# Second mixer of a two-block network: attention in pairs of heads, the dilated half beside the cross projections, rotary scores on 128 rows

## The chip, the cores and the metric

The kernel runs on one NeuronCore of a Trainium2 chip. The metric is the device time of one execution in microseconds. PE is TensorE, DVE VectorE, ACT ScalarE, POOL GpSimd, SP the queue that issues most DMAs.

## The reference

Two blocks run one after the other over 256 latent tokens of width 1024, all in float32. The change touches only the mixer of the second block, which starts by one wide projection and then has two kinds of attention, eight heads each; their outputs are joined, projected and added:

```
proj = h @ w_in                       # h = rmsnorm(x), 1024 -> 3008 columns
q_nope, q_rope, c_kv, k_rope, q_idx, k_idx, w_idx, qkv = split(proj)   # rope() on q_rope, k_rope, q_idx, k_idx
q_lat = einsum('bshn,hnc->bshc', q_nope, w_uk)
index = einsum(relu(q_idx . k_idx), w_idx)        # 8 index heads, causal
sel   = top_k(index, 64)                          # per query
s     = (q_lat . c_kv[sel] + q_rope . k_rope[sel]) * 96 ** -0.5
o_a   = (softmax(s) @ c_kv[sel]) @ w_uv           # sparse attention, 8 heads
# dilated attention, 8 heads of 64: windows (128,1), (512,4), (2048,16), causal,
# the three outputs weighted by the softmax of their log denominators
o_b   = dilated_attention(rope(q_b), rope(k_b), v_b)
x     = x + concat(o_a, o_b) @ w_out
# then: cross attention over 256 memory tokens, an MLP, a final norm
```

With weights from the log denominators, the dilated attention is one softmax over all causal keys in which a key counts as often as it lies in a window.

## The kernel before

Activations stand transposed, features on the 128 partitions and tokens in the free dimension. All large projections go through one stream of weight blocks (128 x 1024 float32, 512 KB). SP loads block n + 4 once DVE is done with block n; ACT copies a block to a rounded high part (`split`, L1434), DVE subtracts for the low part (`low`, L1890), and PE adds three products, high x high, high x low, low x high (`tile`, L597 to L599, 24 matmuls of 256 columns; `moving`, L1038 to L1040, 12 of 512 columns). ACT and DVE prepare a block three blocks ahead (`lead`). Every engine has its own program, and within an engine everything runs in the order in which the code is written; semaphores join the engines. So the order of the work is what each of the four programs says.

The second mixer goes in five stretches:

- `in2`: 22 tiles of the input projection, copied by ACT into `proj` (PJ);
- `in2_v`: four blocks for the dilated values, then the norm of the latent `kv2`;
- a loop over `SIDE` = 16 weight blocks, eight for the cross keys (`xk`) and eight for the cross values (`xv`). Beside the blocks stand, by the step j: two rotations (`rotate`, L1053) at j under 8, four index products (L1144) with ACT's relu and DVE's weighted sum at j = 4 to 7, top-k rounds on DVE (L2414 to L2417) at j = 8 to 15, latent queries (L1152) at j = 10 to 13;
- `attend(DSA)`: the sparse attention, 16 steps, one head and 128 queries each;
- `attend(DIL)`: the dilated attention, 16 steps.

A step a of `attend` is: PE the scores of a (L1162 and L1163, or L1185), the transposes of the probabilities of a - 2 (L1077), the values of a - 3 (L1169 or L1190); DVE scale and mask (L2354), maximum (L2356), negation (L2357), then for a - 1 the reciprocal and the scaling of the probabilities (L2365, L2366); ACT the exponential (L1789, L1787) and the copy of the transposed probabilities (L1795). In the dilated attention DVE also multiplies by the count of windows and sums (L2364). A step always takes all 256 keys. The rotary part of the sparse scores has 32 features, so its product uses 32 rows of PE; four heads lie above each other in one tile, and so does the rotary key, four times:

```
mm(o[:, 0:SEQ], QL[:, h, q], PJ[:, 6, :], start=True, stop=False)
return mm(o[:, 0:SEQ], PJ[po:po + 32, 4 + h // 4, q], PJ[po:po + 32, 7, :], start=False, stop=True)
```

The last stretch is followed by the output projection `out2`, which takes each 128 features when their low part is there.

## Time and profile before

| | |
|---|---|
| runs | 1772.07, 1773.58, 1779.05 us (median 1773.58) |
| profiled execution | 1773.6 us, its span 1771.7 us |
| PE busy | 1664.0 us (94%), 11578 matmuls |
| DVE, ACT, POOL busy | 1145.7 (65%), 800.2 (45%), 111.4 us (6%) |
| chain that ended last | PE 85%, DVE 8%, ACT 3%, issue 2%, DMA 1% |
| DMA | 230.72 MB, mean 130 GB/s |

The share of PE is an average over stages that differ. A window gives, for one stretch, how long each engine was busy and the mean granted clock of PE, where 1.00 is 2.4 GHz and 0.50 is 1.2 GHz. A busy PE at 0.50 does half the work of one at 1.00. Each timeline row is an instruction, or several alike merged, with its start and length; matmuls overlap, so what one costs is the distance between starts. In brackets stands how long the engine was idle before, and for whom.

### The profile page before, as it was taken

How to read it: one execution, taken by the hardware profiler on the slowest of the kernel's cores; microseconds unless marked ns; L12 is line 12 of the kernel's file. 1: busy time of each engine (PE TensorE's matmuls, PEld its weight loads, DVE VectorE, ACT ScalarE, POOL GpSimd, SP SyncE). 2: the span in 40 equal slices, each digit the busy share in tenths (PEclk: the TensorE clock that was granted, in tenths of full speed). 3: DMA queues.
4: the chain of work that ended last, by engine and by line, in shares of the span. 5: the costliest groups of instructions: out<-in, count | busy, mean ns of one | idle time of the engine just before them, and what ended most of it. 6: DMA issues, size and time to landing. Idle time of an engine off the chain costs nothing.

```text
span 1771.7 us, 31774 instructions
## 1 busy us (share of the span) xinstructions
PE 1664.0 (94%) x11578; PEld 1420.7 (80%) x11578; DVE 1145.7 (65%) x2011; ACT 800.2 (45%) x1434; POOL 111.4 (6%) x124
## 2 busy tenths in 40 slices
PE   7999968888989999999899999999999999999998
PEld 1688867788867777788786699999987557899998
DVE  0678464455489999966545468875559665567643
ACT  2556422223354444422364457764444434556542
POOL 1000033040100000001000010001000001010000
PEclk9999888889989999999899999999999877999999
DMA  8355310000245555555342045566453202345553
GB/s 351 112 189 193 103 31 2 1 3 1 84 131 186 181 184 183 178 181 175 122 143 72 1 127 186 186 207 209 145 176 111 68 1 84 108 134 187 189 188 96
DMA packets 62841, 230.72 MB, mean 130 GB/s; under 512 B 6753, under 2 KB 8033, under 8 KB 62241
## 3 DMA queue, kind: packets, MB, share of 16 engines
q1 hardware_dynamic: 61344, 223.37, 38.8%
q0 software_dynamic: 1120, 5.80, 1.0%
q8 instruction: 61, 1.00, 0.2%
q10 hardware_dynamic: 288, 0.33, 0.1%
q14 instruction: 28, 0.22, 0.0%
HBM read 228.43 MB, written 1.05 MB: 130 GB/s over the span
## 4 chain that ended last, share of the span: by engine, by line
PE 85%; DVE 8%; ACT 3%; issue 2%; DMA 1%; POOL 0%; DVEq 0%; ACTq 0%; SPq 0%; POOLq 0%
PE proj L597 21%; PE proj L599 20%; PE proj L598 20%; PE bank L1077 1%; DVE w_low L1890 1%; DMA a_first<-a_head 1%; PE bank L649 1%; PE proj L672 1%; PE bank L1190 1%; PE bank L843 1%; PE bank L860 1%; PE bank L1185 1%; PE bank L1096 1%; PE proj L1038 1%; PE bank L863 1%
## 5 line engine op out<-in xcount | busy, mean ns | idle before, releaser
L597 PE MATMUL proj<-h_high,w_high 128*128 128x256 f32 (+1 forms) x1768 | 583.2, 330 | 22.7 <-DVE h_low L1923 12.3
L599 PE MATMUL proj<-h_high,w_low 128*128 128x256 f32 (+1 forms) x1768 | 573.5, 324 | 0.0
L598 PE MATMUL proj<-h_low,w_high 128*128 128x256 f32 (+1 forms) x1768 | 573.2, 324 | 0.0
L1890 DVE TENSOR_TENSOR w_low<-w_raw,w_high 128x1024 fp32r<-128x1024 f32 x322 | 393.2, 1224 | 221.2 <-ACT w_high L1434 219.9
L1434 ACT ACTIVATE w_high<-w_raw 128x1024 fp32r<-128x1024 f32 x322 | 338.1, 1055 | 244.7 <-PE proj L599 237.4
L597 PEld LDWEIGHTS proj<-h_high,w_high 128*128 128x128 f32 x1768 | 338.9, 192 | 65.3 <-issue 18.9
L599 PEld LDWEIGHTS proj<-h_high,w_low 128*128 128x128 f32 x1768 | 339.4, 192 | 27.3
L598 PEld LDWEIGHTS proj<-h_low,w_high 128*128 128x128 f32 x1768 | 338.9, 192 | 25.5
L599 PE MATMUL proj<-act_high,w_low 128*128 128x256 f32 (+1 forms) x608 | 189.9, 312 | 0.0
L597 PE MATMUL proj<-act_high,w_high 128*128 128x256 f32 (+1 forms) x608 | 189.4, 311 | 0.4 <-DVE w_low L1890 0.4
L598 PE MATMUL proj<-act_low,w_high 128*128 128x256 f32 (+1 forms) x608 | 189.5, 312 | 0.0
L597 PEld LDWEIGHTS proj<-act_high,w_high 128*128 128x128 f32 x608 | 114.1, 188 | 8.2 <-DVE w_low L1890 0.8
L598 PEld LDWEIGHTS proj<-act_low,w_high 128*128 128x128 f32 x608 | 113.8, 187 | 7.7
L599 PEld LDWEIGHTS proj<-act_high,w_low 128*128 128x128 f32 x608 | 114.3, 188 | 6.6
L1510 ACT ACTIVATE conv_in<-proj 128x512 f32<-128x512 f32 (+1 forms) x100 | 49.9, 499 | 118.9 <-PE proj L599 115.9
L2008 DVE SCALAR_TENSOR_TENSOR mod_products<-a_ring,cond_rows 128x1024 f32<-128x1024 f32 x80 | 103.0, 1287 | 0.0
L1321 POOL TENSOR_TENSOR tmp<-tmp 128x256 f32<-128x256 f32 (+1 forms) x40 | 44.2, 1111 | 893.7 <-ACT tmp L1450 715.8
L2008 DVE SCALAR_TENSOR_TENSOR a_ring<-a_ring,cond_rows 128x1024 f32<-128x1024 f32 x80 | 97.5, 1219 | 0.0
L1972 DVE SCALAR_TENSOR_TENSOR conv_mid<-conv_in,cols_sb,conv_mid 128x512 f32<-128x512 f32 (+1 forms) x100 | 63.5, 635 | 14.0 <-DVE conv_mid L1970 8.2
L1970 DVE SCALAR_TENSOR_TENSOR conv_mid<-conv_in,cols_sb,conv_mid 128x512 f32<-128x512 f32 (+1 forms) x100 | 63.2, 632 | 11.6 <-ACT conv_mid L1511 9.9
L1511 ACT ACTIVATE conv_mid<-proj,cols_sb 128x512 f32<-128x512 f32 (+1 forms) x100 | 58.8, 588 | 0.0
L1642 ACT ACTIVATE lev_m<-bank 128x256 f32<-128x256 f32 (+1 forms) x48 | 18.3, 384 | 87.7 <-PE bank L843 63.6
(382 smaller groups left out, 2048.8 us busy)
## 6 DMA issues: line engine op xcount, KB each, us to landing
w_raw<-w_stream SPq DMA_DIRECT2D x322, 512.0 KB, 3.6
a_ring<-a_stream SPq DMA_DIRECT2D x80, 512.0 KB, 3.7
a_first<-a_head SPq DMA_DIRECT2D x4, 2048.0 KB, 20.2
x<-x_in SPq DMA_DIRECT2D x1, 2048.0 KB, 13.3
late_tab<-late_tables POOLq DMA_DIRECT2D x1, 1664.0 KB, 7.6
cond_rows<-cond_rows SPq DMA_DIRECT2D x1, 1024.0 KB, 18.6
cond_rows<-cond_rows POOLq DMA_DIRECT2D x1, 1024.0 KB, 5.1
x<-mem_in POOLq DMA_DIRECT2D x1, 1024.0 KB, 6.0
```

The lines of the kernel that those rows point to most:

```text
L597: mm(out_, wh, xh, start=first, stop=False)
L598: mm(out_, wh, xl, start=False, stop=False)
L599: return mm(out_, wl, xh, start=False, stop=last)
L1321: nc.gpsimd.tensor_tensor(squares(name, 0), squares(name, 0), squares(name, k), ALU.add).then_inc(n_early, 1)
L1434: f(wh(n), RAW[:, n % 4, :], ACT.Copy).then_inc(w_high, 1)
L1510: f(XP[:, k % 2, 0:n, 1:SEQ + 1], PL[t % 2][:, 0:width].rearrange("p (s t) -> p s t", s=n), ACT.Copy)
L1511: f(C1[:, k % 2, 0:width], PL[t % 2][:, 0:width], ACT.Identity, scale=C[:, ds(taps + 3 * k + 1 + 3 * per * it, 1)]).then_inc(tile_out, 1)
L1642: f(M1[x, k % 2, :, :], BK[k % 2][x, 0:4 * 64].rearrange("p (h j) -> p h j", h=HEADS), ACT.Copy).then_inc(G["lv_m1"], 1)
L1890: v.tensor_tensor(wl(n), RAW[:, n % 4, :], wh(n), ALU.subtract).then_inc(w_low, 1)
L1970: v.scalar_tensor_tensor(o, XP[:, k % 2, 0:n, 0:SEQ], C[:, ds(taps + 3 * k + 3 * per * it, 1)], o, ALU.mult, ALU.add).then_inc(conv_mid, 1)
L1972: v.scalar_tensor_tensor(o, XP[:, k % 2, 0:n, 2:SEQ + 2], C[:, ds(taps + 3 * k + 2 + 3 * per * it, 1)], o, ALU.mult, ALU.add).then_inc(con ...
L2008: v.scalar_tensor_tensor(o, w, 1.0, cond[:, s, :], ALU.mult, ALU.mult, accum_out=MODF[:, ds(2 * (A_FIRST + j) + s + 2 * off, 1)]).then_inc ...
```

## The change

- The columns of the input projection are put in another order: index queries, index key and weights first, then latent, rotary parts, dilated queries and keys, and the sparse queries last. A rotation follows each of the input tiles from m = 2 on, two tiles behind (`rope_at`). The norm's second half, the index products in pairs and the transpose of the latent go beside the four `in2_v` blocks; the other index products and the latent queries beside the first four cross-key blocks.
- Both attentions go two heads per step (`PairLayer`, `pair_step`), eight steps each; steps of the first 128 queries take only 128 keys. The index sums and top-k rounds do the same.
- The top-k rounds move to j = 4 to 11, and the dilated attention is placed beside the blocks from j = 4 (`DIL_AT`). The sparse attention is alone behind them.
- The count of windows goes into the mask as its logarithm, and DVE's product and the table of counts go.
- The rotary key is copied by POOL into four tiles that are zero outside of 32 rows (`KM`); the rotary scores take all 128 rows of a query tile against the copy of their head.
- `out2` waits for all heads of the sparse attention at once.

```diff
-                           rows(np.where(count > 0, 0, NEG)), rows(count)], axis=1).astype(f)
+                           rows(np.where(count > 0, np.log(np.maximum(count, 1)), NEG))], axis=1).astype(f)
...
-    w_in2 = np.concatenate([w2[:, 0:896], np.tile(w2[:, 896:928], (1, 4)), np.tile(w2[:, 1440:1504], (1, 2)),
-                            wide(w2[:, 1504:1512]), w2[:, 928:1440], w2[:, 1512:2536]], axis=1)
+    w_in2 = np.concatenate([w2[:, 928:1440], np.tile(w2[:, 1440:1504], (1, 2)), wide(w2[:, 1504:1512]), w2[:, 768:896],
+                            w2[:, 512:768], np.tile(w2[:, 896:928], (1, 4)), w2[:, 1512:2536], w2[:, 0:512]], axis=1)
...
+        KM = place("rope_key_rows", [P, 4, SEQ])
...
+        SX = place("scores", [P, 2, 2, SEQ])
...
+        class PairLayer:
+
+            def __init__(self, name, a0, e0, scale):
+                self.name, self.a0, self.e0, self.scale = name, a0, e0, scale
+                self.n, self.per, self.lag = 8, 4, 9 if name == "dsa" else 7
+                self.steps = self.n - self.per + self.lag + 1
+
+                self.pairs = [(0, 4), (1, 5), (2, 6), (3, 7)] if name == "dsa" else [(0, 2), (1, 3), (4, 6), (5, 7)]
...
         SIDE = 16
-        ROTATE_AT = {j: [r for r in (2 * j, 2 * j + 1) if r < len(ROPE2)] for j in range(SIDE)}
-        INDEX_AT, TOP_AT, LATENT_AT = range(4, 8), range(8, 16), range(10, 14)
+        TOP_AT, DIL_AT = range(4, 12), 4
...
+            def pair_step(ly, a, scores, values):
...
+                if a < ly.n:
...
+                    pe.wait_ge(A["at_m"], ly.a0 + max(0, a - 1))
+                    for i in range(2):
+                        last = scores(ly.pairs[a // 2][i], a % 2, BK[a % 2][:, i * SEQ:i * SEQ + (1 + a % 2) * P])
+                    last.then_inc(A["at_s"], 1)
+                if 2 <= a < ly.n + 2:
+                    p = a - 2
+                    nk = 1 + p % 2
+                    pe.wait_ge(A["at_n"], ly.a0 + p + 1)
+                    for i in range(2):
+                        for k in range(nk):
+                            at = i * SEQ + k * P
+                            last = nc.tensor.transpose(BK[2 + p % 2][:, (i * nk + k) * P:(i * nk + k + 1) * P], PB[:, p % 3, at:at + P], ID[:])
+                    last.then_inc(A["at_t"], 1)
+                if 3 <= a < ly.n + 3:
+                    p = a - 3
+                    e, nk = p // 2, 1 + p % 2
+                    pe.wait_ge(A["at_pt"], ly.a0 + p + 1)
...
+                    for i in range(2):
+                        last = values(ly.pairs[e][i], p % 2, PT[:, p % 2, i * nk:(i + 1) * nk, :], nk)
+                    last.then_inc(A["at_o"], 1)
...
+            def dil_scores(h, qt, o):
+                q, po = slice(qt * P, (qt + 1) * P), 64 * (h % 2)
+                return mm(o, PJ[po:po + 64, QB + h // 2, q], PJ[po:po + 64, KB + h // 2, 0:(1 + qt) * P], start=True, stop=True)
+
+            def dil_values(h, qt, pt, nk):
+                po, at = 64 * (h % 2), h // 2 % 2 * SEQ + qt * P
+                for k in range(nk):
+                    last = mm(BK[4 + h // 4][po:po + 64, at:at + P], VBK[:, k, h * 64:(h + 1) * 64], pt[:, k, :], start=(k == 0), stop=(k == nk - 1))
+                return last
...
+            def index_logits(b):
+
+                for c in index_at(b):
...
+                    po, w = 64 * (h % 2), (1 + c // 8) * P
+                    if c >= 2:
+                        pe.wait_ge(A["ix_r"], c - 1)
+                    mm(index_bank(c)[:, 0:w], PJ[po:po + 64, QI + h // 2, qt * P:(qt + 1) * P], PJ[po:po + 64, KI, 0:w], start=True, stop=True).then_inc(A["ix_l"], 1)
...
+            first_tiles("in2", LAT, SEQ, h_ready("mix"))
+            for m in range(2, 22):
                 tile(B0["in2"] + m, T0["in2"] + m, LAT, SEQ)
-            moving("in2_v", HH, HL, SEQ, range(4), 2, 4)
-            norm("kv2")
+                rotate(ROPE2, r1, rope_at(m))
...
+            norm_sum("kv2")
+            for b in range(4):
+                moving("in2_v", HH, HL, SEQ, (b,), 2, 4)
+                if b == 0:
+                    norm_spread("kv2")
+                if b == 2:
+                    pe.wait_ge(n_xn, NORM_C0["kv2"] + 1)
+                    for qt in range(2):
+                        last = nc.tensor.transpose(BK[5][:, qt * P:(qt + 1) * P], PJ[:, LAT_KV, qt * P:(qt + 1) * P], ID[:])
+                    last.then_inc(A["ct_t"], 1)
+                index_logits(b)
...
+                index_logits(4 + j)
+                if j < 4:
...
+                if j >= DIL_AT:
+                    pair_step(DIL, j - DIL_AT, dil_scores, dil_values)
...
+            pe.wait_ge(A["km_done"], 4)
...
+                q, k = slice(qt * P, (qt + 1) * P), slice(0, (1 + qt) * P)
+                mm(o, QL[:, h, q], PJ[:, LAT_KV, k], start=True, stop=False)
+                return mm(o, PJ[:, QR + h // 4, q], KM[:, h % 4, k], start=False, stop=True)
...
+            def dsa_out(pair):
...
+                pe.wait_ge(A["ol_out"], pair + 1)
+                po = 64 * (pair % 2)
+                for i in range(2):
+                    last = mm(PL[pair // 2][po:po + 64, i * SEQ:(i + 1) * SEQ], WUV[:, DSA.pairs[pair][i], :], OL[:, pair % 2, i, :], start=True, stop=True)
+                last.then_inc(A["ol_o"], 1)
+
+            for a in range(DSA.n + 3):
+                pair_step(DSA, a, dsa_scores, dsa_values)
+                if a >= 6 and a % 2 == 0:
+                    dsa_out((a - 6) // 2)
+            dsa_out(3)
+
+            project("out2", LAT, SEQ, lambda k: (A["at_y"], DSA.e0 + 2))
...
+            nc.gpsimd.memset(KM[:], 0.0).then_inc(A["km_zero"], 1)
+            pool.wait_ge(A["km_zero"], 1)
+            pool.wait_ge(A["rp_d"], len(ROPE1) + ROPE2_TILES.index(KRP) + 1)
+            for i in range(4):
+                rows = slice(32 * i, 32 * i + 32)
+                nc.gpsimd.tensor_copy(KM[rows, i, :], PJ[rows, KRP, :]).then_inc(A["km_done"], 1)
...
+            def pair_step(ly, a, out_bank, out_chunk):
+                if a < ly.n:
+                    r, w = a % 3, (1 + a % 2) * P
+                    act.wait_ge(A["at_m"], ly.a0 + a + 1)
+
+                    act.wait_ge(A["at_t"], ly.a0 + max(0, a - 2))
+                    for i in range(2):
+                        last = f(PB[:, r, i * SEQ:i * SEQ + w], SX[:, a % 2, i, 0:w], ACT.Exp, bias=SA[:, 1, r, i:i + 1], accum_out=SA[:, 2, r, i:i + 1])
+                    last.then_inc(A["at_p"], 1)
+                if 2 <= a < ly.n + 2:
+                    p = a - 2
+                    nk = 1 + p % 2
+                    act.wait_ge(A["at_t"], ly.a0 + p + 1)
+                    act.wait_ge(A["at_o"], ly.a0 + p - 1)
+                    f(PT[:, p % 2, 0:2 * nk, :], BK[2 + p % 2][:, 0:2 * nk * P].rearrange("p (k q) -> p k q", k=2 * nk), ACT.Copy).then_inc(A["at_pt"], 1)
...
+                if j >= DIL_AT:
+                    pair_step(DIL, j - DIL_AT, lambda e: BK[4 + e][:].rearrange("p (c q) -> p c q", c=2), lambda h, e: h[:, 4 + 2 * e:6 + 2 * e, LAT])
+            for a in range(DSA.steps):
+                pair_step(DSA, a, lambda e: PL[e][:].rearrange("p (c q) -> p c q", c=2), lambda h, e: h[:, e:e + 3:2, LAT])
...
+            def pair_step(ly, a, out_bank, out_chunk, mask):
+                if a < ly.n:
+                    r, w = a % 3, (1 + a % 2) * P
+                    sx = SX[:, a % 2, :, 0:w]
+                    dve.wait_ge(A["at_s"], ly.a0 + a + 1)
+                    link(v.scalar_tensor_tensor(sx, BK[a % 2][:].rearrange("p (i k) -> p i k", i=2)[:, :, 0:w], ly.scale, mask(a % 2)[:, 0:w].unsqueeze(1).to_broadcast([P, 2, w]), ALU.mult, ALU.add))
+                    link(v.tensor_reduce(SA[:, 0, r, :], sx, AXES.X, ALU.max))
+                    v.tensor_scalar(SA[:, 1, r, :], SA[:, 0, r, :], -1.0, None, ALU.mult).then_inc(A["at_m"], 1)
+                if 1 <= a <= ly.n:
+                    p = a - 1
+                    r, w = p % 3, (1 + p % 2) * P
+                    dve.wait_ge(A["at_p"], ly.a0 + p + 1)
+                    link(v.reciprocal(SA[:, 3, r, :], SA[:, 2, r, :]))
+                    pb = PB[:, r, :].rearrange("p (i k) -> p i k", i=2)[:, :, 0:w]
+                    v.tensor_tensor(pb, pb, SA[:, 3, r, :].unsqueeze(2).to_broadcast([P, 2, w]), ALU.mult).then_inc(A["at_n"], 1)
...
                 if j == TOP_AT[0]:
                     dve.wait_ge(A["ix_a"], 16)
...
                 if j in TOP_AT:
 
-                    v.max(M8[:, 0, :], IX[:, 0, :])
+                    v.max(M8[:, 0, :], IX[:, 0, 0:P])
                     link(v.max(M8[:, 1, :], IX[:, 1, :]))
-                    v.match_replace(IX[:, 0, :], M8[:, 0, :], IX[:, 0, :], TAKEN)
+                    v.match_replace(IX[:, 0, 0:P], M8[:, 0, :], IX[:, 0, 0:P], TAKEN)
                     link(v.match_replace(IX[:, 1, :], M8[:, 1, :], IX[:, 1, :], TAKEN))
...
+                if j >= DIL_AT:
+                    pair_step(DIL, j - DIL_AT, lambda e: BK[4 + e][:].rearrange("p (c q) -> p c q", c=2), lambda h, e: h[:, 4 + 2 * e:6 + 2 * e, LAT],
+                              lambda qt: ltab("dneg", qt))
+            for a in range(DSA.steps):
+                pair_step(DSA, a, lambda e: PL[e][:].rearrange("p (c q) -> p c q", c=2), lambda h, e: h[:, e:e + 3:2, LAT], lambda qt: AM[:, qt, :])
```

The names in the listings that follow are tiles: `w_high` and `w_low` the parts of a weight block, `probs` the probabilities, `bank` and `proj` PSUM banks (`proj` as a source is PJ). ACT beside cross-key blocks before, two steps of the loop with index work:

```order
L1434 ACTIVATE w_high<-w_raw 128x1024
L1834 ACTIVATE cross_k<-proj 128x256
L1850 ACTIVATE relu<-bank 128x256 x4
L1434 ACTIVATE w_high_145<-w_raw 128x1024
L1834 ACTIVATE cross_k<-proj 128x256
```

ACT beside cross-key blocks now, from j = 6:

```order
L1946 ACTIVATE cross_k<-proj 128x256
L1880 ACTIVATE probs,pair_small<-scores,pair_small 128x128 x2
L1887 ACTIVATE probs_t<-bank 128x256
L1511 ACTIVATE w_high_147<-w_raw 128x1024
L1946 ACTIVATE cross_k<-proj 128x256
L1880 ACTIVATE probs,pair_small<-scores,pair_small 128x256 x2
L1887 ACTIVATE probs_t<-bank 128x512
```

The exponentials and the copy of the dilated attention now stand between two weight blocks.

DVE beside a cross-value block before, one top-k round between two blocks:

```order
L1890 TENSOR_TENSOR w_low<-w_raw,w_high 128x1024
L2414 MAX max_137<-index 128x8
L2415 MAX max_137<-index 128x8
L2416 MATCH_REPLACE index<-max_137,index 128x256
L2417 MATCH_REPLACE index<-max_137,index 128x256
L1890 TENSOR_TENSOR w_low_146<-w_raw,w_high_145 128x1024
```

DVE now, beside a block at j = 4 to 11:

```order
L1996 TENSOR_TENSOR w_low_148<-w_raw,w_high_147 128x1024
L2543 MAX max_137<-index 128x8
L2544 MAX max_137<-index 128x8
L2545 MATCH_REPLACE index<-max_137,index 128x128
L2546 MATCH_REPLACE index<-max_137,index 128x256
L2476 SCALAR_TENSOR_TENSOR scores<-bank,late_tab 128x512
L2477 TENSOR_REDUCE pair_small<-scores 128x2
L2478 TENSOR_SCALAR pair_small<-pair_small 128x2
L2483 RECIPROCAL pair_small<-pair_small 128x2
L2485 TENSOR_TENSOR probs<-probs,pair_small 128x2x128
L1996 TENSOR_TENSOR w_low<-w_raw,w_high 128x1024
```

Five instructions of a dilated step stand behind the top-k round and ahead of the next block.

PE in the sparse attention before, one step:

```order
L1162 MATMUL bank<-proj,q_lat 128x256
L1163 MATMUL bank<-proj 128x256
L1077 MATMUL bank<-ident_sb,probs 128x128 x2
L1169 MATMUL bank<-probs_t,c_tok 128x128 x2
L1162 MATMUL bank<-proj,q_lat 128x256
```

PE now, one step of two heads:

```order
L1242 MATMUL bank<-proj,q_lat 128x256
L1243 MATMUL bank<-rope_key_rows,proj 128x256
L1242 MATMUL bank<-proj,q_lat 128x256
L1243 MATMUL bank<-rope_key_rows,proj 128x256
L1129 MATMUL bank<-ident_sb,probs 128x128 x4
L1248 MATMUL bank<-probs_t,c_tok 128x128 x2
```

Two heads' scores stand together; the values behind them are of an earlier step with 128 keys.

## Rows read from the trace of the kernel before

**Rows 1.** Windows of the second mixer's five stretches: us, busy time (count) by engine, PEclk the granted clock.
```profile
1243.30:1307.80 64.50, 64.50 (x528) 64.49 (x529) 34.58 (x43) 31.78 (x49) 0.00 (x0) 0.96 0.53 164
1307.80:1322.40 14.60, 12.78 (x61) 10.19 (x60) 5.14 (x7) 7.24 (x12) 0.00 (x0) 1.00 0.63 184
1322.40:1387.60 65.20, 62.63 (x372) 50.41 (x370) 57.18 (x127) 28.82 (x53) 0.00 (x0) 1.00 0.39 128
1387.60:1434.20 46.60, 45.28 (x176) 26.07 (x176) 25.84 (x90) 18.40 (x60) 0.00 (x0) 0.82 0.04 12
1434.20:1480.10 45.90, 42.59 (x130) 23.37 (x129) 31.00 (x116) 13.89 (x36) 0.00 (x0) 0.56 0.00 1
```

**Rows 2.** Windows of 4 us, and one of the first mixer's attention.
```profile
970.00:975.00 5.00, 5.00 (x24) 2.73 (x25) 1.99 (x5) 1.96 (x6) 0.00 (x0) 1.00 0.01 3
1384.00:1388.00 4.00, 3.27 (x15) 2.31 (x13) 3.90 (x12) 2.70 (x4) 0.00 (x0) 1.00 0.38 131
1392.00:1396.00 4.00, 4.00 (x12) 2.22 (x11) 2.43 (x8) 1.30 (x5) 0.00 (x0) 0.50 0.00 0
1412.00:1416.00 4.00, 4.00 (x20) 2.28 (x19) 2.46 (x10) 1.42 (x6) 0.00 (x0) 1.00 0.00 0
...
1456.00:1460.00 4.00, 4.00 (x12) 2.02 (x12) 2.22 (x9) 0.83 (x3) 0.00 (x0) 0.50 0.00 0
```

**Rows 3.** Timeline of PE in an index tile: start, us, engine, line, what, [idle before].
```profile
1340.25 1.02 PE L1053 MATMUL bank<-proj,late_tab 128*128 128x256 f32 x4
1341.20 0.70 PE L1144 MATMUL bank<-proj 64*128 64x256 f32 x4
1342.37 0.97 PE L1144 MATMUL bank<-proj 64*128 64x256 f32 x4 [0.47 <-ACT relu L1850]
...
1346.20 1.03 PE L1053 MATMUL bank<-proj,late_tab 128*128 128x256 f32 x4
```

**Rows 4.** Timeline of DVE beside the cross values.
```profile
1382.88 1.23 DVE L1890 TENSOR_TENSOR w_low<-w_raw,w_high 128x1024 fp32r<-128x1024 f32 x1 [0.79 <-ACT w_high L1434]
1384.03 0.42 DVE L2414 MAX8 max<-index 128x8 f32<-128x256 f32 x1
...
1385.72 1.22 DVE L1890 TENSOR_TENSOR w_low<-w_raw,w_high 128x1024 fp32r<-128x1024 f32 x1
```

**Rows 5.** Timeline of DVE in the sparse attention.
```profile
1390.73 0.42 DVE L2354 SCALAR_TENSOR_TENSOR scores<-bank,top_mask 128x256 f32<-128x256 f32 x1
...
1391.64 0.15 DVE L2357 TENSOR_SCALAR small<-small 128x1 f32<-128x1 f32 x1
```

**Rows 6.** Timeline of ACT beside the values and in the sparse attention.
```profile
1384.20 1.06 ACT L1434 ACTIVATE w_high<-w_raw 128x1024 fp32r<-128x1024 f32 x1 [1.42 <-PE proj L1040]
...
1427.69 0.51 ACT L1789 ACTIVATE probs<-scores,small 128x256 f32<-128x256 f32 x1 [1.47 <-DVE small L2357]
...
1428.20 0.36 ACT L1795 ACTIVATE probs_t<-bank 128x256 f32<-128x256 f32 x1
```

**Rows 7.** Instructions by form, first mixer's attention: line, what, xcount | busy, mean ns | idle.
```profile
L1795 ACT ACTIVATE probs_t<-bank 128x512 f32<-128x512 f32 x15 | 8.8, 588 | 0.0
...
L2356 DVE TENSOR_REDUCE small<-bank 128x1 f32<-128x512 f32 x11 | 7.6, 692 | 13.3 <-PE bank L1092 13.3
```

**Rows 8.** Timeline of PE in the sparse attention at full clock.
```profile
1412.99 0.70 PE L1162 MATMUL bank<-proj,q_lat 128*128 128x256 f32 x2
1413.62 0.69 PE L1163 MATMUL bank<-proj 32*128 32x256 f32 x2
1414.24 0.44 PE L1077 MATMUL bank<-ident_sb,probs 128*128 128x128 f32 x2
1414.52 0.61 PE L1169 MATMUL bank<-probs_t,c_tok 128*128 128x128 f32 x4
1414.96 0.60 PE L1162 MATMUL bank<-proj,q_lat 128*128 128x256 f32 x2
1415.49 0.69 PE L1163 MATMUL bank<-proj 32*128 32x256 f32 x2
```

More of the change, by code:

```diff
@@ L440, in two_blocks_kernel @@
         PT = place("probs_t", [P, 2, 4, P])
-        SX = place("scores", [P, 2, SEQ])
+        SX = place("scores", [P, 2, 2, SEQ])
         RT = place("rot", [P, 2, SEQ])
@@ L1062, in _, with attend @@
             pe.wait_ge(tile_out, T0["out1"] + 2)
-            def attend(ly, scores, values, extra=None):
+            def attend(ly, scores, values):
                 nb = len(ly.banks)
@@ L1165, in dsa_values @@
-            def dsa_values(h, qt, pt):
-                if qt == 0 and h >= 2:
-                    pe.wait_ge(A["ol_out"], h - 1)
-                for k in range(2):
-                    last = mm(BK[4 + h % 2][:, qt * P:(qt + 1) * P], CTK[:, k, :], pt[:, k, :], start=(k == 0), stop=(k == 1))
-                return last
-            def dsa_out(h):
-                pair, po = h // 2, 64 * (h % 2)
-                pe.wait_ge(A["ol_out"], h + 1)
-                if h % 2 == 0 and pair >= 2:
-                    pe.wait_ge(A["at_y"], DSA.e0 + pair - 1)
-                mm(PL[pair % 2][po:po + 64, 0:SEQ], WUV[:, h, :], OL[:, h % 2, :], start=True, stop=True).then_inc(A["ol_o"], 1)
@@ L1822, in _ @@
             norm_high("mix")
-            project("in2", copy_to("in2", PJF, SEQ), 5)
-            for m in (20, 21):
+            for m in range(22):
                 split(B0["in2"] + m + lead("in2"))
@@ L1827, in _, with index_relu @@
                 f(PJ[:, m, :], PL[(T0["in2"] + m) % 2][:, 0:SEQ], ACT.Copy).then_inc(tile_out, 1)
[L1828 to L1829 removed]
+            def index_relu(b):
+                for c in index_at(b):
+                    w = (1 + c // 8) * P
+                    act.wait_ge(A["ix_l"], c + 1)
+                    if c >= 2:
+                        act.wait_ge(A["ix_a"], c - 1)
+                    f(RL[:, c % 2, 0:w], index_bank(c)[:, 0:w], ACT.Relu).then_inc(A["ix_r"], 1)
+            norm_start("kv2")
+            square("kv2", 0, (tile_out, T0["in2"] + LAT_KV + 3))
+            for b in range(4):
+                split(B0["in2_v"] + b + lead("in2_v"))
+                if b == 0:
+                    norm_root("kv2")
+                if b == 3:
+                    for m in range(2):
+                        t = T0["in2_v"] + m
+                        done(t)
+                        f(VBK[:, m, :], PL[t % 2][:], ACT.Copy).then_inc(tile_out, 1)
+                    act.wait_ge(A["ct_t"], 1)
+                    f(CTK[:], BK[5][:, 0:SEQ].rearrange("p (k c) -> p k c", k=2), ACT.Copy).then_inc(A["ct_out"], 1)
+                index_relu(b)
             for j in range(SIDE):
@@ L2409, in _ @@
+                index_sum(b)
+            for j in range(SIDE):
+                low((B0["xk"] + j if j < 8 else B0["xv"] + j - 8) + lead("xk"))
+                index_sum(4 + j)
                 if j == TOP_AT[0]:
                     dve.wait_ge(A["ix_a"], 16)
-                    link(v.tensor_tensor(IX[:], IX[:], causal, ALU.add))
+                    for qt in range(2):
+                        ins = v.tensor_tensor(IX[:, qt, 0:(1 + qt) * P], IX[:, qt, 0:(1 + qt) * P], causal[:, qt, 0:(1 + qt) * P], ALU.add)
+                    link(ins)
```

249 lines of the change are left out of this document (116 added, 133 removed).

## The prediction, made before the change was run

> **What bounds the kernel now.** I read the page first (busy shares and the chain that ended last), then the windows by stage, and last the timelines of single engines. On the page PE is 94% busy and 85% of the chain. The second mixer runs from 1243.3 to 1480.1 us, 236.8 us in five stretches [rows 1]: the input projection (64.5), its value block with the latent norm (14.6), the cross keys and values with rotations, indexer and latents beside them (65.2), the sparse attention (46.6) and the dilated attention (45.9). The reader is to see that in the last two PE is busy 45.28 and 42.59 us while its granted clock averages 0.82 and 0.56: they are bound by PE at half clock. In 4 us pieces the clock is 0.50 with PE busy all 4 us, goes back to 1.00 in the middle of the sparse attention, and never in the dilated one [rows 2]. ACT's exponentials wait for DVE (1.47 us ahead of one [rows 6]), but PE runs through that time, so it costs nothing.
>
> The profiled execution took 1773.6 us, 1.9 more than its span of 1771.7, and equals the median of the runs (1773.58). I sum against 1773.6.
>
> **The input projection, 64.5 to 72.2.** Its 22 tiles stay. Sixteen rotations come in after the tiles. Two of them take 0.95 us on PE (1340.25 to 1341.20 [rows 3]), so 16 x 0.48 = 7.7 is added. DVE has 1.15 for a weight block [rows 4] and three steps of a rotation, each like the 0.42 of [rows 5], 2.4 of a tile's 3.4 us, so it stays hidden; without that cover each tile would wait for DVE.
>
> **Values and norm, 14.6 to 16.1.** The second half of the norm moves behind a weight block; of the 1.8 us that PE is idle there (14.6 less 12.78 [rows 1]) I take 1.2 as gone. It waits for the sum until DVE has scaled eight chunks of x, which is no worse than before. Added are eight index products of 128 columns. With 256 columns four took 2.07 less a stall of 0.47 (1341.20 to 1343.3 [rows 3]), 0.40 each; with half the columns between 0.20 and 0.40, I take 0.25, so 2.0, and 0.7 for transposes that came later before.
>
> **The first four cross-key tiles, 18.0.** A tile is 2.9 (1343.3 to 1346.20 [rows 3]); two index products and two latents of the same 64-row form at 0.40 come on top: 4.5 each. The chain of four index products with a 0.47 us stall per tile [rows 3] is gone; that, and half the columns for the first 128 queries, is where this part gains.
>
> **The other twelve tiles, with the dilated attention and the top-k beside them, 64.** PE's own work is 12 x 2.9 = 34.8 and the attention of 8 pair steps: scores 4 x (0.6 + 1.1), transposes 3.3, values 4 x (0.6 + 1.2), all between the 64-row products of [rows 3] and the 128-row ones of [rows 8] with something for the 64 columns, together 17.3, so 52.1. But I find a new loop between DVE and ACT, which is longer. ACT makes the high half of a weight block, DVE its low half, DVE then does a top-k round, the masked scores, maximum and negation; ACT must take the exponentials of these and copy transposed probabilities before it comes to the next weight block. Nothing of this overlaps within the loop:
> - DVE's weight block and top-k round are 2.84 from start to start (1382.88 to 1385.72 [rows 4]); for the first 128 queries the round now has 128 columns, and at the 0.27 that lies between 256 and 512 elements of a maximum [rows 5, 7] two instructions save 0.27: 2.57.
> - Scores, maximum, negation: 1.06 for 256 elements (1390.73 to 1391.79 [rows 5]). For 512 the maximum takes 0.692 where 256 took 0.42 [rows 5, 7], so 1.6.
> - ACT: an exponential with its sum is 0.51 for 256 (1427.69 to 1428.20 [rows 6]), I take 0.40 for 128; two are 1.02 or 0.80. The transposed copy holds ACT for 0.29 after 128x256, 0.53 after 128x512 (0.588 against 0.36 [rows 6, 7]). The next high half is 1.06 [rows 6]. With two handovers 2.2 or 2.7.
> Even to odd step: 2.2 + 2.57 + 1.6 = 6.4; odd to even: 2.7 + 2.57 + 1.06 = 6.3. PE needs 4.3 to 5.9 per tile here and waits, through the normalized probabilities, for that loop. The first maximum comes about 5.9 us after the stretch begins, seven loops are 44 less 0.8 for the copies that the first two lack, and from the last maximum PE has about 14.3 (four tiles 11.6, last values and transposes, and a wait on the mask): 63.5, I say 64. Bounds: 52.1 if everything hides, and 12 x 6.4 = 77 if every tile is held.
>
> **The sparse attention alone, 31.7.** Two heads share a step. From the stretch at full clock [rows 8]: a 256-column score product 0.63, and 0.53 at its best (1414.96 to 1415.49), I take 0.55 and 0.30 for 128 columns, so four even steps of 4 x 0.30 and four odd ones of 4 x 0.55 are 13.6; 24 transposes at 0.14 are 3.3; 24 value products at 0.22 are 5.3; 8 output products at 0.58 are 4.6. Sum 26.8. Idle: 1.2 at the start for the copies of the cross values, 1.2 until the first probabilities, 1.0 in the tail, and 1.5 before the output projection, which now waits for all its heads and not one by one. DVE's 2.0 to 2.4 per step is under PE's 3.3. The four padded copies are made on POOL, idle here, and their wait ended long before. At half clock the 26.8 would be up to 53.6.
>
> The product with 32 rows took 0.63 and the one with 128 rows beside it 0.63 (1412.99, 1413.62, 1414.24 [rows 8]), so the padding takes nothing off a product as such. The Trainium skill ("TensorEngine Tiling (Array Packing)", Key Properties) says that a change of tiling mode drains TensorE. By it the 32-row product also slowed its neighbour and the all-128-row scores would run at 256 columns in the best 0.53 or a little under; the sum would be 31 instead of 31.7. I do not use it.
>
> **Sum.** 72.2 + 16.1 + 18.0 + 64 + 31.7 = 202.0 against 236.8: -34.8. Nothing before or after the mixer changes but names and counts, and a table that is 256 KB shorter. 1773.6 - 34.8 = 1738.8, say 1739.
>
> **Rivals.** (a) *The loop doesn't hold PE.* The twelve tiles take 52.1: 1727. For it: weights are made three blocks ahead. Against: scores are needed in the same tile, only the weights are ahead; and before, a like exchange between ACT and DVE already held index tiles to one every 5.95 us for 5.5 of PE's work [rows 3]. (b) *The clock falls in the sparse attention*, as it did by 1392 [rows 2]. For it: a start with two idle stretches of 1.2. Against: the first mixer's attention, 128-row and 64-row products of 512 columns, ran at 1.00 throughout [rows 2], and the 32-row products are gone. It costs 8 if the first half of the stage goes at half clock, 26.8 if all: 1747 to 1766, I say 1752. (c) *Slower than before: the clock falls beside the tiles and stays down.* The place is the first dilated steps, where a tile is followed by 64-row products and up to 1.8 us of waiting. At half clock a tile is 5.8 and the attention 4.2: 10.0 x 8, and 29 for the last four, 109 instead of 64; the sparse stage then also starts low, +26.8: +72, 1811. It decides for slower from +34.8, that is with three quarters of the tiles at half clock. Against it: at 1384 to 1388 with PE busy only 3.27 and at all projection tiles the clock is 1.00 [rows 2], and the index tiles with 64-row products and stalls had 1.00 as well [rows 1]. A short fall in some tiles, +6 to +16 (1745 to 1755), is likelier than this.
>
> The Trainium skill ("TensorE: Matmul & The Clock Gate", Why this matters for your kernels) asks that matmuls follow each other without long pauses to keep the full clock. By that rule (b) and (c) could not happen, since no pause is long; this trace disagrees, with 0.50 at PE busy 4.00 of 4.00 us [rows 2]. So I leave (b) its chance.
>
> **Numbers.** Forecast 1739, with its own range 1732 to 1746, chance 0.45; (a) 0.17; (b) 0.20; a short fall beside the tiles 0.14; (c) 0.03; the rest 0.01 near no change. Eight in ten lie between 1723 (rival (a) with a little less in the sparse stage) and 1758 (rival (b) at more than its middle). What a measurement here can tell from no change is 0.5%, 8.9 us, so faster means below 1764.7: all cases but (c), the rest and the far end of (b). Faster 0.95, same 0.02, slower 0.03.
>
> **What would show it.** The five stretches of the profile after should be near 72, 16, 18, 64 and 32. Tiles beside the dilated scores should come every 6.3 to 6.4 us, with PE waiting 1 to 2 us before a transpose for the probabilities, DVE idle 1.5 to 2 us before its weight block for ACT, and ACT idle only before exponentials. A period of 5 means (a). A granted clock under 0.9 in the last stretch means (b), under 0.8 in the fourth the fall beside the tiles. The forecast is wrong if the fourth stretch is under 57 or over 71, or the last over 38.

## The result, and the profile after

The changed kernel took 1738.34 us (median of four, 1736.91 to 1740.02) against 1773.83 (four runs, 1772.07 to 1779.05) for the kernel before; ratio 0.978, 95% interval 0.976 to 0.980. The forecast was 1739. The profiled execution took 1738.19 us with a span of 1736.0. The mixer runs from 1242.52 to 1444.05 us: 201.5 instead of 236.8. Its five stretches, cut as those of [rows 1] (us, busy time and count of PE, its weight loads, DVE, ACT, POOL, then granted clock, DMA share, GB/s):

```profile
1242.52:1314.45 71.93, 71.93 (x562) 70.86 (x562) 51.30 (x89) 31.52 (x50) 2.43 (x4) 0.96 0.48 154
1314.45:1330.94 16.49, 14.79 (x75) 11.29 (x75) 8.83 (x16) 7.12 (x17) 0.00 (x0) 1.00 0.40 128
1330.94:1347.24 16.30, 16.30 (x129) 14.26 (x129) 8.38 (x12) 10.09 (x26) 0.00 (x0) 1.00 0.40 130
1347.24:1411.28 64.04, 54.99 (x298) 42.27 (x296) 43.45 (x109) 27.85 (x65) 0.00 (x0) 0.97 0.31 100
1411.28:1444.05 32.77, 24.81 (x154) 19.85 (x153) 17.14 (x43) 15.91 (x49) 0.00 (x0) 1.00 0.04 14
```

| stretch | before | forecast | after |
|---|---|---|---|
| input projection | 64.5 | 72.2 | 71.9 |
| values, norm | 14.6 | 16.1 | 16.5 |
| first four cross tiles | in 65.2 | 18.0 | 16.3 |
| twelve tiles with top-k and dilated attention | in 65.2, and 45.9 | 64 | 64.0 |
| sparse attention | 46.6 | 31.7 | 32.8 |

The two attentions, which ran at 0.82 and 0.56 before, now run at 1.00 and, between the tiles, 0.97. One short fall is left; two windows of 4 us with it, and one of the sparse attention, answer to [rows 2]:

```profile
1364.00:1368.00 4.00, 2.19 (x12) 1.46 (x11) 2.50 (x7) 2.36 (x7) 0.00 (x0) 0.90 0.36 128
1368.00:1372.00 4.00, 4.00 (x13) 2.94 (x12) 3.83 (x12) 0.36 (x1) 0.00 (x0) 0.67 0.39 130
...
1416.00:1420.00 4.00, 2.90 (x19) 2.65 (x20) 3.34 (x10) 2.24 (x9) 0.00 (x0) 1.00 0.02 6
```

The clock fell near 1367, after PE had waited 1.35 and 1.81 us in two steps, and was back by 1371. It cost some 1.7 us (a tenth of 4 and a third of 4), an estimate from these two windows.

The loop that the forecast found is there. Start, length, engine, line, and in brackets the idle time before and whom it was for; the second turn, from one negated maximum of the dilated scores to the next:

```profile
1359.32 0.17 DVE L2478 TENSOR_SCALAR pair_small<-pair_small 128x2 f32<-128x2 f32 x1
...
1359.53 0.51 ACT L1880 ACTIVATE probs<-scores,pair_small 128x256 f32<-128x256 f32 x1 [3.99 <-DVE pair_small L2478]
...
1360.53 1.05 ACT L1511 ACTIVATE w_high<-w_raw 128x1024 fp32r<-128x1024 f32 x1
...
1361.61 1.22 DVE L1996 TENSOR_TENSOR w_low<-w_raw,w_high 128x1024 fp32r<-128x1024 f32 x1 [1.59 <-ACT w_high L1511]
...
1363.73 0.41 DVE L2546 MATCH_REPLACE8 index<-max,index 128x256 f32<-128x256 f32 x1
1364.17 0.42 DVE L2476 SCALAR_TENSOR_TENSOR scores<-bank,late_tab 128x256 f32<-128x256 f32 x1
...
1365.09 0.17 DVE L2478 TENSOR_SCALAR pair_small<-pair_small 128x2 f32<-128x2 f32 x1
...
1366.11 0.66 PE L1129 MATMUL bank<-ident_sb,probs 128*128 128x128 f32 x4 [1.81 <-DVE probs L2485]
```

DVE's negated maximum (1359.32) releases ACT's exponentials, these let ACT come to the next weight block (1360.53), that releases DVE's low half (1361.61, after 1.59 of idling), and only behind it and the top-k round (its last replacement at 1363.73) come the next scores, with the next negation at 1365.09: 5.77 us. This turn is the shortest, since there is no transposed copy for ACT yet; from the third on, with the copy, a turn takes 6.24 or 6.35. In all the eight negations stand between 1353.2 and 1396.6, 6.2 us apart. PE waits 1.81 us before the transposes at 1366.11, the longest of its waits for probabilities; the others are 0.3 to 1.35. What PE waited for in this stretch, in us, times and longest:

```profile
PE bank L1129 <- DVE probs L2485: 6.7, 7, 1.8
PE bank L1180 <- ACT probs_t L1887: 1.7, 3, 0.6
```

In the sparse attention (score products of 128 and 256 columns, and the two idle pieces of a pair of steps; a product is recorded as two instructions, so `x2` is one product, while a transpose is one):

```profile
1412.75 0.39 PE L1243 MATMUL bank<-rope_key_rows,proj 128*128 128x128 f32 x2
1412.97 0.60 PE L1242 MATMUL bank<-proj,q_lat 128*128 128x256 f32 x2
1413.40 0.59 PE L1243 MATMUL bank<-rope_key_rows,proj 128*128 128x256 f32 x2
...
1421.50 0.44 PE L1129 MATMUL bank<-ident_sb,probs 128*128 128x128 f32 x2 [0.46 <-DVE probs L2485]
1422.57 1.16 PE L1248 MATMUL bank<-probs_t,c_tok 128*128 128x128 f32 x8 [0.64 <-ACT probs_t L1887]
```

A 256-column score product on 128 rows now takes 0.43 (1412.97 to 1413.40) where the 32-row one took 0.63 [rows 8], and one of 128 columns 0.22.

### The profile page after: what moved, and what is told of

The parts are those of the page before. It is cut to its first block, busy times and chain, and to the rows that moved or that the text cites. A ratio compares the mean times of both kernels' runs of the same rounds, so it can differ in the third digit from the quotient of the medians.

```text
span 1736.0 us, 31397 instructions
## 1 busy us (share of the span) xinstructions
PE 1618.5 (93%) x11530; PEld 1402.4 (81%) x11530; DVE 1120.7 (65%) x1898; ACT 791.0 (46%) x1426; POOL 114.5 (7%) x129
## 4 chain that ended last, share of the span: by engine, by line
PE 81%; DVE 10%; ACT 4%; issue 3%; DMA 1%; POOL 0%; DVEq 0%; ACTq 0%; POOLq 0%
PE proj L624 21%; PE proj L626 20%; PE proj L625 20%; DVE w_low L1996 2%; PE bank L699 1%; PE bank L676 1%; ACT w_high L1511 1%; PE proj L699 1%; PE bank L870 1%; PE bank L887 1%; PE bank L1153 1%; PE bank L890 1%; PE bank L722 1%; PE bank L1149 1%; PE bank L1104 1%
```

## The experiments

Every experiment was run by turns with the kernel before, but not all on the same chip: the kernel before took 1778.9 beside the first four, 1778.2 beside the next four and 1773.6 beside the last two. So two experiments compare by their ratios rather than by their medians, and best by the stretch that the edit touches. In the windows of the experiments the fourth stretch ends with the first sparse score, 0.7 us later than in the table above: 64.7 and 32.1 for the changed kernel.

**Rotary scores on 32 rows again.**

```diff
-                return mm(o, PJ[:, QR + h // 4, q], KM[:, h % 4, k], start=False, stop=True)
+                return mm(o, PJ[po:po + 32, QR + h // 4, q], PJ[po:po + 32, KRP, k], start=False, stop=True)
```

> The changed kernel, but the rotary scores of the sparse attention use 32 rows again (the four copies of the key are still made). Theory: the sparse stretch of 32.8 us is bound by handovers between PE, ACT and DVE and ran at a granted clock of 1.00, and a product of 32 rows cost as much as one of 128: 1738, within 2 us, clock 1.00. Rival one, the change of rows costs each neighbour: 32 products at 0.05 to 0.1, 1740 to 1742. Rival two, the 32-row products were what the clock fell by: the granted clock of the sparse stretch goes to 0.5 to 0.8 as before the change, 1746 to 1762.

Measured: 1749.51 us (1747.03 to 1753.68), ratio 0.984 [0.982, 0.986]. The two last stretches and a window of 4 us:

```profile
1346.68:1411.41 64.73, 54.99 (x298) 42.18 (x296) 43.45 (x109) 28.51 (x67) 0.00 (x0) 0.97 0.31 103
1411.41:1454.53 43.12, 39.09 (x153) 25.41 (x153) 17.41 (x43) 15.35 (x48) 0.00 (x0) 0.76 0.01 6
1416.00:1420.00 4.00, 4.00 (x12) 2.48 (x11) 2.41 (x6) 1.09 (x4) 0.00 (x0) 0.50 0.00 2
```

The fourth is unchanged, the sparse one takes 43.1 instead of 32.1, with the clock at 0.50 in the middle. In the five runs the clock granted over the whole kernel was 0.948 to 0.950, against 0.953 to 0.955 in the four of the changed kernel, so the fall is not of one execution. The theory fell, and the second rival held. The first held too, at 0.2 a product where it had 0.05 to 0.1, as this piece at full clock shows:

```profile
1431.80 0.69 PE L1243 MATMUL bank<-proj 32*128 32x256 f32 x2
1432.43 0.70 PE L1242 MATMUL bank<-proj,q_lat 128*128 128x256 f32 x2
...
1434.94 0.48 PE L1243 MATMUL bank<-proj 32*128 32x128 f32 x2
1435.35 0.49 PE L1242 MATMUL bank<-proj,q_lat 128*128 128x128 f32 x2
```

A 32-row product of 256 columns takes 0.63 and one of 128 columns 0.41, where the 128-row ones take 0.43 and 0.22 (above), and the products beside them are slowed alike. So the padded key is worth 11 us here, by the clock and by shorter products together; how much each has in the 11 this run can't say.

**The top-k rounds left out.** The edit removes the four maximum and replacement instructions of a step on DVE; the sparse attention then doesn't pick the reference's keys, and only the time counts.

> The changed kernel without its eight top-k rounds (maximum and replacement on DVE are left out, so the selection is not the reference's). Theory: the rounds stand in the loop DVE, ACT, DVE that holds the twelve tiles of the fourth stretch. Without the 1.5 us the loop drops from 6.05 to about 4.6 and PE's own work (4.3 and 5.9 per tile) is the bound: the stretch falls from 64.0 to 54 to 57, 1729 to 1732. Rival: PE's chain through the probabilities holds the tiles whatever DVE does beside them, the stretch stays over 61: 1735 to 1738.

Measured: 1729.62 us (1727.20 to 1730.10), ratio 0.972 [0.970, 0.975].

```profile
1348.70:1402.15 53.45, 52.64 (x298) 41.17 (x297) 32.50 (x61) 28.63 (x67) 0.00 (x0) 1.00 0.37 125
```

53.5 instead of 64.7: the loop held the tiles, and PE is now busy 52.6 of the 53.5. The clock stays at 1.00, so the 1.7 us of the short fall, which came after two waits in the loop, are among the 11.3.

**The pair step ahead of the top-k round.**

```diff
                 low((B0["xk"] + j if j < 8 else B0["xv"] + j - 8) + lead("xk"))
+                if j >= DIL_AT:
+                    pair_step(DIL, j - DIL_AT, ...)
                 if j in TOP_AT:
...
-                if j >= DIL_AT:
-                    pair_step(DIL, j - DIL_AT, ...)
```

> The changed kernel with one edit on DVE: the pair step of the dilated attention stands ahead of the top-k round instead of behind it. Theory of the loop: ACT can take the exponentials and the next weight block (2.1 to 2.7 us) while DVE normalizes and does the round (2.1 to 2.3), so the loop drops by about 1.4 and the result is that of leaving the rounds out: fourth stretch 54 to 58, 1729 to 1733. Rival: it only moves the wait, since DVE then comes to the next weight block 1.5 us later and PE waits for weights: 1737 to 1740.

Measured: 1729.03 us (1727.32 to 1730.57), ratio 0.972 [0.970, 0.974]. A turn of the loop now, and the two last stretches:

```profile
1366.76 0.17 DVE L2478 TENSOR_SCALAR pair_small<-pair_small 128x2 f32<-128x2 f32 x1
...
1366.97 0.51 ACT L1880 ACTIVATE probs<-scores,pair_small 128x256 f32<-128x256 f32 x1 [2.62 <-DVE pair_small L2478]
...
1368.36 0.41 DVE L2549 MATCH_REPLACE8 index<-max,index 128x256 f32<-128x256 f32 x1
1368.44 1.04 ACT L1511 ACTIVATE w_high<-w_raw 128x1024 fp32r<-128x1024 f32 x1
...
1369.59 1.22 DVE L1996 TENSOR_TENSOR w_low<-w_raw,w_high 128x1024 fp32r<-128x1024 f32 x1 [0.82 <-ACT w_high L1511]
...
1371.64 0.17 DVE L2478 TENSOR_SCALAR pair_small<-pair_small 128x2 f32<-128x2 f32 x1
```

```profile
1347.90:1401.80 53.90, 52.71 (x298) 41.18 (x296) 42.71 (x109) 28.63 (x67) 0.00 (x0) 1.00 0.37 123
1401.80:1435.36 33.56, 26.28 (x152) 20.93 (x153) 17.14 (x43) 15.25 (x48) 0.00 (x0) 0.95 0.02 8
```

The round (its last replacement at 1368.36) now runs while ACT takes the exponentials, and the next scores follow the low half (1369.59) at once. This turn is 4.88 us (1366.76 to 1371.64) and has the transposed copy; its like in the changed kernel (1371.44 to 1377.68) took 6.24. The round costs next to nothing in this place: 53.9 against 53.5 without it. The last stretch has a short fall in it (0.95), at 1426 to 1429.

**The dilated attention alone, behind all sixteen blocks.** The three `pair_step(DIL, ...)` calls move out of the loop over blocks, into one of their own ahead of the sparse attention.

> The changed kernel with its dilated attention behind the sixteen weight blocks and not beside them. Twelve tiles at 2.9 are 35; the dilated pairs alone have 17 us of PE work and, by the sparse stretch (32.8 for 24.8 of work), handovers of 1 us a step. Theory: being beside the blocks gained little, since the loop gave most of it back: 35 + 26 = 61 to 64, total 1736 to 1741. Rival one: the blocks hid all the handovers of the attention and more, 35 + 34: 1744 to 1748. Rival two: alone, the clock falls to 0.50 as in the dilated attention before, +17 and more: 1755 to 1765.

Measured: 1739.12 us (1736.94 to 1744.95), ratio 0.978 [0.975, 0.980]. Blocks, dilated, sparse:

```profile
1353.98:1387.78 33.80, 33.80 (x194) 29.21 (x192) 27.51 (x68) 16.25 (x23) 0.00 (x0) 1.00 0.56 186
1387.78:1418.65 30.87, 28.66 (x105) 20.01 (x104) 15.75 (x41) 13.35 (x43) 0.00 (x0) 0.56 0.05 18
1418.65:1450.73 32.08, 24.80 (x154) 19.84 (x153) 17.05 (x43) 15.41 (x48) 0.00 (x0) 1.00 0.00 1
```

33.8 + 30.9 = 64.7, what both together take in the changed kernel. The profiled execution is the longest of the four, but its surplus lies ahead of these windows: the first begins 6.7 us later than in the changed kernel. The total was as the theory said, the reason was not: alone, the clock falls to 0.56 (the second rival, though not at its price), and half clock and handovers together cost as much there as the loop does beside the blocks.

**The same with all 128 rows in the dilated scores.** The scores are then sums over two heads.

```diff
-                return mm(o, PJ[po:po + 64, QB + h // 2, q], PJ[po:po + 64, KB + h // 2, 0:(1 + qt) * P], start=True, stop=True)
+                return mm(o, PJ[:, QB + h // 2, q], PJ[:, KB + h // 2, 0:(1 + qt) * P], start=True, stop=True)
```

> The changed kernel with the dilated attention alone behind the blocks, and its scores on all 128 rows (not padded, so the dilated outputs are not the reference's). With 64 rows this stretch took 30.9 us from its first score to the first sparse score, at 0.50 nearly throughout. Theory (rows decide): 1.00 and 24 to 27 us, so 4 to 7 less than that run: 1732 to 1735. Rival: 0.50 stays, within 2 of it: 1737 to 1741.

Measured: 1735.86 us (1734.48 to 1736.68). The ratio, 0.9775 [0.975, 0.980], is that of the run above, so the totals don't tell the two apart; the stretch does:

```profile
1382.58:1408.05 25.47, 18.94 (x105) 13.91 (x103) 15.49 (x41) 13.28 (x43) 0.00 (x0) 0.90 0.07 22
```

25.5 instead of 30.9 at 0.90 instead of 0.56, inside the theory's 24 to 27, though not at its 1.00: a fall began at 1403, after waits of 1.22 and 0.64, and ended by 1410. In this execution another short fall, at 1433 to 1437, stands in the sparse attention behind it (34.4 against 32.1).

**The kernel before with the padded key alone.** The copies on POOL and their wait as in the change, and:

```diff
-                return mm(o[:, 0:SEQ], PJ[po:po + 32, 4 + h // 4, q], PJ[po:po + 32, 7, :], start=False, stop=True)
+                return mm(o[:, 0:SEQ], PJ[:, 4 + h // 4, q], KM[:, h % 4, :], start=False, stop=True)
```

> The kernel before with one part of the change alone: four zero-padded copies of the rotary key and rotary scores on 128 rows, still 256 keys a step. Theory (products of 32 rows among PE's work are what the granted clock falls by in the sparse attention): its stretch goes from 0.82 to 1.00 and from 46.6 to 36 to 40 us, while the dilated one keeps 0.56: 6 to 11 us less than the kernel before. Rival: the clock falls there because PE has work all the time without a pause (busy 4.00 of 4.00), whatever the rows: within 3 us of the kernel before, clock 0.8.

Measured: 1765.83 us (1761.83 to 1770.74), ratio 0.994 [0.993, 0.996], 7 to 13 us less. Sparse and dilated:

```profile
1386.39:1424.04 37.65, 34.97 (x176) 23.71 (x176) 25.71 (x89) 18.35 (x60) 0.00 (x0) 1.00 0.05 15
1424.04:1469.92 45.88, 43.33 (x129) 23.64 (x128) 31.13 (x116) 13.88 (x36) 0.00 (x0) 0.54 0.00 1
```

46.6 became 37.65 at a clock of 1.00, with PE still busy 35.0 of it; the dilated attention is the same to 0.1 us. The rival fell: near to steady work on all rows kept the full clock. Two steps with their output product take 4.41 us at full clock (1403.73 to 1408.14) where they took 4.60 (1412.99 [rows 8] to 1417.59). By that the shorter products are 8 x 0.19 = 1.5 of the 9.0, since PE gives most of what they save back in waits, and the clock is the rest; this is an estimate.

**And the dilated scores on 128 rows too,** with the same edit as above, so that the dilated outputs are sums over two heads.

> As the run beside it, and the dilated scores take all 128 rows too. The keys are not padded, so these scores are sums over two heads and the dilated outputs are not the reference's; only the time counts. Theory: the dilated stretch (45.9 us at 0.56) goes to a clock of 1.00 and 28 to 34 us, 18 to 28 us less than the kernel before in all. Rival: its 64-column value products, or steady work as such, hold the clock at 0.50, and it stays over 42: no more than the run beside it.

Measured: 1756.22 us (1754.75 to 1759.35), ratio 0.989 [0.987, 0.992]. Sparse, dilated, and two windows of the latter:

```profile
1391.07:1428.75 37.68, 34.99 (x177) 23.73 (x177) 25.71 (x89) 18.38 (x60) 0.00 (x0) 1.00 0.04 15
1428.75:1465.06 36.31, 28.36 (x130) 16.30 (x129) 30.08 (x116) 13.90 (x36) 0.00 (x0) 0.91 0.00 1
1432.00:1436.00 4.00, 3.02 (x10) 1.83 (x10) 3.69 (x15) 1.48 (x5) 0.00 (x0) 0.55 0.00 0
```

The dilated stretch goes from 45.9 to 36.3. The fall after the first waits is still there (0.55), but now the clock is back by 1440 and stays. The gain is smaller than expected, 28 to 34 for the stretch: at full clock PE waits for DVE's probabilities (7.1 us in 14 waits over the stretch), and DVE is busy 30.1 of 36.3. There DVE still has the count product and takes one head per step; what each of the two costs was not tried.

**Better versions.** Three steps of the sparse attention beside the last value blocks, on top of the reordered top-k:

```diff
+                if j >= 13:
+                    pair_step(DSA, j - 13, dsa_scores, dsa_values)
...
-            for a in range(DSA.n + 3):
+            for a in range(3, DSA.n + 3):
```

> A kernel meant to be better: top-k round behind the pair step (1729.0), and the first three steps of the sparse attention beside the last three value blocks (j = 13 to 15) instead of behind them. Theory: the idle 1.3 us ahead of the first transposes and the 0.7 for the copies of the cross values find cover, and the scores of three steps go from a stretch bound by handovers to one with PE's tiles: 1725 to 1727. Rival: the scores only add their 3.5 us of PE work to tiles that PE already fills, and the masks are late: 1728 to 1731.

Measured: 1729.46 us (1726.92 to 1731.45), ratio 0.974 [0.972, 0.977], against 0.972 of the kernel it builds on: nothing gained.

```profile
1345.76:1403.55 57.79, 56.45 (x324) 44.80 (x322) 45.51 (x117) 30.28 (x75) 0.00 (x0) 1.00 0.33 110
1403.55:1432.72 29.17, 22.64 (x127) 17.07 (x127) 14.33 (x36) 13.34 (x40) 0.00 (x0) 0.94 0.06 19
```

57.8 + 29.2 = 87.0 against 53.9 + 33.6 = 87.5. What left the last stretch came into one where PE was already full; the rival held.

Then ACT's copy of the transposed probabilities ahead of the exponentials of the step, also on top of the reordered top-k:

```diff
             def pair_step(ly, a, out_bank, out_chunk):
-                if a < ly.n:
-                    ...                       # exponentials of a
                 if 2 <= a < ly.n + 2:
                     ...                       # copy of the transposed probabilities of a - 2
+                if a < ly.n:
+                    ...
```

> A kernel meant to be better: top-k round behind the pair step (1729.0, sparse stretch 33.6 us), and ACT copies the transposed probabilities of two steps back ahead of the exponentials of this step, not behind them. Theory (the sparse stretch is bound by handovers, and ACT idles for DVE's maximum when the copy could be made): the four waits of PE for the copy (2.2 us) go and some of those for the probabilities (4.1), 28 to 31 us, 1724 to 1727. Rival: the exponentials come later by what the copy takes, and DVE and PE behind them: 1728 to 1731.

Measured: 1726.12 us (1722.66 to 1729.09), ratio 0.972 [0.969, 0.974]. Sparse stretch, and the place at which PE waited 0.64 for the copy:

```profile
1404.60:1433.94 29.34, 24.00 (x152) 19.75 (x153) 17.14 (x43) 15.73 (x48) 0.00 (x0) 1.00 0.02 7
```

```profile
1414.12 0.44 PE L1129 MATMUL bank<-ident_sb,probs 128*128 128x128 f32 x2 [0.46 <-DVE probs L2485]
1414.39 1.06 PE L1248 MATMUL bank<-probs_t,c_tok 128*128 128x128 f32 x8
```

29.3, and no wait between transposes and values. The run it builds on has 33.6 with a short fall in it (0.95); against the changed kernel's 32.1 at the same 1.00 the copy is worth 2.7. In the totals it is 3 us by the medians and 1 by the ratios, with overlapping intervals: shown by the stretch, not by the runs.

And the first tile of the output projection begins with the chunks that are there:

```diff
-            project("out2", LAT, SEQ, lambda k: (A["at_y"], DSA.e0 + 2))
+            order = [4, 5, 6, 7, 0, 2, 1, 3]
...
+                        pe.wait_ge(A["at_y"], DSA.e0 + (2 if k in (1, 3) else 1))
```

The two PSUM banks of the sparse outputs change places with it (`PL[1 - ...]` on PE, ACT and DVE), so that this tile can start in the one that is free first.

> As the run beside it, and the first output-projection tile takes the four dilated chunks and two sparse ones as soon as half of the sparse heads are done, in the bank that these free. Theory: the 1.5 us that PE waits for the last low parts find cover under 2.1 us of products: 1.3 to 1.5 less than the run beside it, 1722.5 to 1725.5. Rival: the wait reappears ahead of chunks 1 and 3, since ACT's and DVE's last steps are not earlier: no difference.

Measured: 1722.49 us (1720.31 to 1728.39), ratio 0.970 [0.968, 0.973]; the best here, 14 us (by the ratios) to 16 (by the medians) under the changed kernel. The end of the sparse attention in the changed kernel and in this one:

```profile
1440.71 1.83 PE L1256 MATMUL proj<-o_lat,w_uv_sb 128*64 128x256 f32 x8
1444.05 0.35 PE L624 MATMUL proj<-h_high,w_high 128*128 128x256 f32 x1 [1.50 <-DVE h_low L2489]
```

```profile
1425.12 1.83 PE L1256 MATMUL proj<-o_lat,w_uv_sb 128*64 128x256 f32 x8
1426.89 0.39 PE L624 MATMUL proj<-h_high,w_high 128*128 128x256 f32 x1
```

The 1.50 us of waiting are gone and do not come back within the tile: the rival fell. 1.3 to 1.5 was expected; the medians of the two runs beside each other differ by 3.6 and their intervals overlap. The stretch is 27.8 instead of 29.3, so 1.5 of it is the edit's. In the two profiled executions the sparse attention begins at 1404.60 and 1399.11, 5.5 us apart, though nothing ahead of it was changed, so totals vary by more than this edit is worth.

## Why the prediction was right, point by point

The total came out to 1 us partly by luck: the parts were 0.3 and 1.7 too large and 0.4 and 1.1 too small, and these errors cancel. The loop, the one mechanism the forecast rests on, is not luck: leaving the round out and moving it test it by itself.

- **What bounds the kernel** (PE at half clock in both attentions): right, and the runs on the kernel before show what 128 rows alone are worth there: 9.0 us in the sparse stretch, 9.6 in the dilated one.
- **Input projection and values**: 72.2 and 16.1 forecast, 71.9 and 16.5 measured. A rotation cost PE 0.46 (7.4 for 16) and DVE hid its part (busy 51.3 of 71.9).
- **First four tiles, 18.0**: 16.3. The term that was too large is the 64-row product of 256 columns: two of them take 0.54 on PE now, 0.27 each, where 0.40 was taken from four in whose row PE also waits for ACT [rows 3]. The two of a pair stand in different halves of the rows; a 128-row product of the same columns takes 0.43.

```profile
1333.89 0.70 PE L1192 MATMUL bank<-proj 64*128 64x256 f32 x4
1334.43 0.60 PE L1228 MATMUL bank<-proj,w_uk_sb 64*128 64x256 f32 x4
```

- **The loop, 64**: 64.0, and its parts as well: first maximum after 5.9 (its negation measured at 6.0, 1353.2), seven turns in 43.2 (43.4), then 14.3 (14.7). A turn was forecast at 6.3 to 6.4 and is 6.24 to 6.35 with the copy, 6.08 and 5.77 in the two without it. Leaving the round out and moving it both gave about 53.5, which is rival (a)'s 52.1 with what PE really needs. That rival was the right price for a kernel without the loop.
- **The sparse attention, 31.7**: 32.8, from two errors that partly cancel. PE's work was sized at 26.8 and PE was busy 24.8, mainly since the score products were taken at 0.55 and 0.30 and are 0.43 and 0.22 (3.2 less for 32 of them; the 1.2 that this leaves was not followed). The sentence "the padding takes nothing off a product as such" was the step that failed: it read the 32-row product and its neighbour at 0.63 as the price of any product, and they slow each other. Idle time was sized at 4.9 and is 8.0, because two pairs of steps wait 0.46 for probabilities and 0.64 for their copy, 2.2 in all, and the tail waits 1.35, 0.64 and 0.24 where 1.0 was taken. The Trainium skill ("TensorEngine Tiling (Array Packing)", Key Properties) says that a change of tiling mode drains TensorE. The trace of the 32-row run fits it, in a larger size than was worked out from it: 0.63 against 0.43 on either side of the change.
- **Rival (b), the clock falls in the sparse attention**: it didn't, and the reason given ("the 32-row products are gone") is shown by the run that brought them back: 1749.5, inside that rival's 1747 to 1766 and near its 1752.
- **Rival (c) and the short fall**: the short fall came, at 1.7 us, and the 64-row products between the tiles did not hold the clock down.

The Trainium skill ("TensorE: Matmul & The Clock Gate", Why this matters for your kernels) asks for matmuls without long pauses. I had set it against the trace. The runs bear out a part of it: several falls begin after or within waits of PE (1.35 and 1.81 us in the changed kernel before 1367, 0.85 and 1.20 in the dilated stretch of the kernel before with 128 rows). But they don't begin after every such wait (1.34 us at the start of the sparse attention at 1.00), and with 32-row products the clock fell 3 us after a single wait of 0.69, where the changed kernel has the same wait and kept 1.00. How long a fall lasted went with the rows: at the start of the dilated stretch the kernel before has the same two waits (0.85 and 1.21) with 64-row scores as with 128-row ones, and stayed at 0.50 for 41 us with the former, for 7 with the latter.

What stays open: how much of the 11 us of the padded key is clock and how much shorter products; why the clock came back at 1409 in the kernel before [rows 2], with the same 32-row products that it had fallen beside; and what two heads per step and the 128-key steps are worth, since no run takes either of them out alone.

## What to carry to other kernels

Ask of each new instruction on a helper engine which loop it joins, not how busy the engine is: eight rounds of 1.4 us on a DVE that was 68% busy cost about 11 us in one place and next to nothing behind the next step. Before padding an operand looks wasteful, compare products with and without their partial-row neighbours, and read the granted clock of the stretch. When work moves beside other work and the time doesn't change, add up the two stretches apart (33.8 + 30.9) and look for what the neighbourhood cost.

## What the runs showed of the hardware

- In stretches of attention alone whose score products use 32 or 64 of 128 rows the clock fell to 0.50 and stayed there for 17 us (sparse, before and in the 32-row run, both then back at 1.00 beside the same products) and for 27 us and more (dilated, to the end of the stretch or near it); means 0.76 to 0.82 and 0.54 to 0.56. The same stretches with all rows ran at 1.00, 0.90 and 0.91, with PE busy a smaller share of the time, and no fall lasted over 7 us. Between weight tiles of 128 rows the 64-row products ran at 1.00 but for one fall of 3 to 4 us.
- Products of 32 rows next to products of 128: 0.63 each for 256 columns, 0.41 for 128; among products of 128 rows alone 0.43 and 0.22.
- Two products of 64 rows and 256 columns in different halves of the rows: 0.54 for the pair.
